# Retention's output rows and six attention tiles turned by DMA instead of by TensorE

## What is computed

```
ret = retention(rq, rk, rv, rg, pos)        # 4 heads of 128 -> columns 0..511
att = mla(c_q, c_kv, k_pe, ...)             # 4 heads of 128 -> columns 512..1023
x = x + concatenate([ret, att]) @ w_o
h = rmsnorm(x); x = x + (silu(h @ w_gate) * (h @ w_up)) @ w_down
...
# in mla, per head and block of 128 queries, keys up to the query's chunk:
prob = softmax(mask(q_blk @ k^T * scale));  out = prob @ v
```

## Time and profile before

| what | value |
|---|---|
| median of 3 runs | 1220.97 us (1220.86 to 1221.05) |
| the profiled execution's own time | 1221.42 us |
| its span | 1219.8 us |
| TensorE busy | 1209.0 us, 99% |
| VectorE, ScalarE, GpSimd busy | 60%, 40%, 49% |
| granted TensorE clock, mean | 0.999 |

### The profile page before, as it was taken

One profiled execution on the slowest core, in us unless ns is written; L12 is line 12 of the kernel. 1 busy time (PEld: TensorE's weight loads), 2 busy tenths in 40 slices (PEclk: granted clock), 3 DMA queues, 4 the chain that ended last, 5 costly groups with the idle time before them and its releaser, 6 DMA issues.

```text
span 1219.8 us, 16374 instructions
## 1 busy us (share of the span) xinstructions
PE 1209.0 (99%) x5842; PEld 1022.4 (84%) x5842; DVE 731.4 (60%) x1160; ACT 487.4 (40%) x882; POOL 594.7 (49%) x586
## 2 busy tenths in 40 slices
PE   9999999999999999999999999999999999999997
PEld 8888888889998888888888888888888888888886
DVE  5654554476664258645554445544499999967634
ACT  6633333355653135433333333333344334525422
POOL 3567775550010024535543355533499889939211
PEclk9999999999999999999999999999999999999999
DMA  9534322100034200423333233332554555434202
GB/s 338 164 86 79 93 42 61 23 18 18 19 121 139 52 1 1 136 80 123 97 119 102 80 121 99 118 104 78 182 194 158 184 173 190 123 104 84 70 35 104
DMA packets 144239, 125.37 MB, mean 103 GB/s; under 512 B 47008, under 2 KB 110112, under 8 KB 144160
## 3 DMA queue, kind: packets, MB, share of 16 engines
q1 hardware_dynamic: 143728, 123.80, 33.5%
q10 hardware_dynamic: 432, 0.54, 0.2%
HBM read 90.49 MB, written 23.59 MB: 94 GB/s over the span
## 4 chain that ended last, share of the span: by engine, by line
PE 95%; DVE 1%; POOL 1%; ACT 1%; issue 1%; DMA 0%; POOLq 0%; SPq 0%; DVEq 0%; ACTq 0%
PE PS L1816 11%; PE PS L1818 11%; PE PS L1817 11%; PE PS L208 8%; PE PS L210 8%; PE PS L209 8%; PE PS L2151 5%; PE PS L2152 5%; PE PS L2150 5%; PE PS L1120 4%; PE PS L1150 3%; PE PS L2571 2%; PE PS L2573 2%; PE PS L2572 2%; PE PS L2586 2%; PE PS L954 1%
## 5 line engine op out<-in xcount | busy, mean ns | idle before, releaser
L208 PE MATMUL PS<-WF,HTH 128*128 128x512 f32 (+1 forms) x448 | 176.7, 394 | 1.1 <-DVE WF L186 0.8
L210 PE MATMUL PS<-WF,HTL 128*128 128x512 f32 (+1 forms) x448 | 173.1, 386 | 0.0
L209 PE MATMUL PS<-WF,HTH 128*128 128x512 f32 (+1 forms) x448 | 173.0, 386 | 0.0
L1537 DVE TENSOR_TENSOR X<-X,PS 128x512 f32<-128x512 f32 x172 | 110.0, 679 | 51.8 <-PE PS L210 37.2
L1816 PE MATMUL PS<-HTH,WF 128*128 128x512 f32 x336 | 130.7, 389 | 0.0
L1817 PE MATMUL PS<-HTL,WF 128*128 128x512 f32 x336 | 130.7, 389 | 0.0
L1818 PE MATMUL PS<-HTH,WF 128*128 128x512 f32 x336 | 130.7, 389 | 0.0
L1749 DVE TENSOR_TENSOR WF<-RAW,WF 128x512 fp32r<-128x512 f32 x63 | 68.7, 1091 | 77.5 <-ACT WF L1739 77.5
L208 PEld LDWEIGHTS PS<-WF,HTH 128*128 128x128 f32 x448 | 84.2, 188 | 17.0 <-issue 0.8
L1816 PE MATMUL PS<-WF 128*128 128x512 f32 x252 | 98.0, 389 | 0.0
L1817 PE MATMUL PS<-WF 128*128 128x512 f32 x252 | 98.0, 389 | 0.0
(11 more groups left out here) (276 smaller groups left out, 2826.6 us busy)
## 6 DMA issues: line engine op xcount, KB each, us to landing
hid<-TMP SPq DMA_DIRECT2D x74, 256.0 KB, 2.3
TMP<-hid SPq DMA_DIRECT2D x25, 512.0 KB, 4.4
RAW<-in_w_ffn_gate SPq DMA_DIRECT2D x22, 512.0 KB, 4.2
RAW<-in_w_ffn_up SPq DMA_DIRECT2D x22, 512.0 KB, 5.4
RAW<-in_w_ffn_down SPq DMA_DIRECT2D x22, 512.0 KB, 4.3
X<-in_x SPq DMA_DIRECT2D x16, 512.0 KB, 5.7
RAW<-in_w_in SPq DMA_DIRECT2D x32, 256.0 KB, 4.3
TAB<-hid SPq DMA_DIRECT2D x9, 512.0 KB, 4.4
```

What stands on the lines that cost most here:

```text
L208: nc.tensor.matmul(dst, HTH[:, k, tok], w_h, start=(k == 0), stop=False)
L209: nc.tensor.matmul(dst, HTH[:, k, tok], w_l, start=False, stop=False)
L210: last = nc.tensor.matmul(dst, HTL[:, k, tok], w_h, start=False, stop=(k == K - 1))
L1537: nc.vector.tensor_tensor(x, x, src, ALU.add).then_inc(done, 1)
```

## The change

Tiles 6 and 7 of heads 0, 1 and 2 (`by_dma`) are no longer turned by TensorE. GpSimd sorts their words' halves into planes (`late_split`), SP issues a DMA transpose into the one buffer JUNK (`sp_late`), and GpSimd joins them into `P_LATE` (`late_join`); the second DMA waits for the first join, as both land in JUNK. Their values are made in steps 3 and 5 of the next head (`VALUES_AT`). `act_exp` of the next head's tiles 0 and 1 now waits for those two splits instead of for a turn. Retention's eight tiles go the same way through GpSimd and SP, one after the other: three at head 0, one each at heads 1 and 2, three at head 3 (`RET_AT`), each time ahead of that head's `out_weights_lo` in GpSimd's order. Their splits into high part and rest read SBUF instead of PSUM and begin in step 3 of the last head. The first output product stands before the values of tile 30, and the output products use six PSUM banks instead of four. SP issues the second half of `w_o` and the reload of `x` later.

```diff
+        RET_AT = ((0, 1, 2), (3,), (4,), (5, 6, 7))
...
+            head_weights(0)
+            for h in range(HEADS):
+                for t in RET_AT[h]:
+                    sp_retention_turn(e, t)
+                if h < HEADS - 1:
+                    head_weights(h + 1)
+                    sp_late(e, h * T + T - 2)
+                    sp_late(e, h * T + T - 1)
...
+        def by_dma(n):
+
+            return n < (HEADS - 1) * T and n % T >= T - 2
...
+        def late_split(e, n):
+            h, t = n // T, n % T
+            e.wait_ge(a_prob, 2 * n + 2)
...
+            nc.gpsimd.tensor_copy(halves(late_halves(n)[0]), words_of(tmp((t % 2) * 1024, (t + 1) * P))).then_inc(p_words, 1)
+
+        def sp_late(e, n):
...
+            e.wait_ge(p_words, 4 * h + 1 + 2 * i)
+            planes, turned = late_halves(n)
+            e.dma_start_transpose(blocks(turned), planes).then_inc(p_turned[i], 16)
+
+        def late_join(e, n):
+            h, i = n // T, n % 2
+            e.wait_ge(p_turned[i], LATENTS_IN + 16 * (h + 1))
+            planes, turned = late_halves(n)
+            nc.gpsimd.tensor_copy(words_of(P_LATE[i][:, 0:(n % T + 1) * P]), halves(turned)).then_inc(p_words, 1)
...
+                if n == NR - 1:
+                    out_product(e, 0)
+                for v in VALUES_AT[n]:
+                    pe_values(e, v)
+                if not by_dma(n):
+                    pe_turn(e, n)
+            out_product(e, 1)
             pe_values(e, NR - 1)
-            pe_retention_turn(e, (4, 5))
-            out_product(e, 1)
-            pe_retention_turn(e, (6, 7))
...
             if n >= 2:
-                e.wait_ge(a_turn, n - 1)
+                if by_dma(n - 2):
+                    e.wait_ge(p_words, 4 * ((n - 2) // T) + 1 + n % 2)
+                else:
+                    e.wait_ge(a_turn, turns_before(n - 1))
...
             for h in range(HEADS):
+                for t in RET_AT[h]:
+                    retention_turn(e, t)
                 out_weights_lo(e, h)
...
+                if h < HEADS - 1:
+                    late = (h * T + T - 2, h * T + T - 1)
+                    for n in late:
+                        late_split(e, n)
+                    for n in late:
+                        late_join(e, n)
...
+        def retention_turn(e, t):
...
+            nc.gpsimd.tensor_copy(halves(RET_HALVES), words_of(RET[:, t])).then_inc(rt_words, 1)
+            e.wait_ge(rt_turned, 16 * (t + 1))
+            nc.gpsimd.tensor_copy(words_of(RET[:, t]), halves(RET_HALVES_T)).then_inc(rt_words, 1)
...
-            return bank(4 + n % 4 if n >= T else (6, 4, 5, 7)[n % 4])
+            return bank(4 + n % 4 if n >= T else (2, 3, 4, 5, 6, 7, 2, 3)[n])
...
             if n == 0:
                 e.wait_ge(o_w_lo, HEADS)
-                e.wait_ge(a_o_lo, NR - 1)
```

More of the change, by code:

```diff
@@ L1138, in pe_values @@
                 e.wait_ge(a_vh, 1)
[L1139 to L1142, removed]
-            else:
-                e.wait_ge(a_pt, n + 1)
-            if n >= 2:
-                e.wait_ge(a_o_lo, n - 1)
+            p = VALUE_PLACE[n]
+            if p < 2:
+                e.wait_ge(b_qr, 7 + p)
+            if by_dma(n):
+                e.wait_ge(p_words, 4 * h + 3 + n % 2)
+            elif t >= 4:
+                e.wait_ge(a_pt_left, turns_before(n + 1, 4))
+            else:
+                e.wait_ge(a_pt, turns_before(n + 1))
+            if p >= 2:
+                e.wait_ge(a_o_lo, p - 1)
+            turned = P_LATE[n % 2] if by_dma(n) else PT[t % 2]
             for j in range(t + 1):
-                if j == 4:
-                    e.wait_ge(a_pt, n + 1)
-                last = nc.tensor.matmul(bank(6 + t % 2, P), value_part(h, j), PT[t % 2][:, j * P:j * P + P], start=(j == 0),
+                if j == 4 and not by_dma(n):
+                    e.wait_ge(a_pt, turns_before(n + 1))
+                last = nc.tensor.matmul(value_bank(n), value_part(h, j), turned[:, j * P:j * P + P], start=(j == 0),
                                         stop=(j == t))
@@ L1205, in act_out_hi, with turned_copy @@
             h, t = n // T, n % T
-            e.wait_ge(a_pv, n + 1)
-            nc.scalar.copy(HTH[:, h + 4, t * P:t * P + P], bank(6 + t % 2, P)).then_inc(a_o_hi, 1)
+            e.wait_ge(a_pv, VALUE_PLACE[n] + 1)
+            nc.scalar.copy(HTH[:, h + 4, t * P:t * P + P], value_bank(n)).then_inc(a_o_hi, 1)
+        def turned_copy(e, n):
+            t = n % T
+            before = [m for m in range(n) if not by_dma(m) and m % 2 == n % 2]
+            if before:
+                e.wait_ge(a_pv, VALUE_PLACE[before[-1]] + 1)
+            left = min(t + 1, 4) * P
+            right = (t + 1) * P - left
+            if right:
+                e.wait_ge(a_turn_left, turns_before(n + 1, 4))
+                nc.scalar.copy(PT[t % 2][:, 0:left], bank(4)).then_inc(a_pt_left, 1)
+            e.wait_ge(a_turn, turns_before(n + 1))
+            dst, src = (PT[t % 2][:, left:left + right], bank(5, right)) if right else (PT[t % 2][:, 0:left], bank(4, left))
+            nc.scalar.copy(dst, src).then_inc(a_pt, 1)
         def act_3b(e):
@@ L1218, in act_3b @@
                     queries_hi(e, h + 1, t // 2)
[L1219 to L1224, removed]
+                for v in VALUES_AT[n]:
+                    act_out_hi(e, v)
                 if t in (4, 5):
                     out_weights_hi(e, h, t - 4)
[L1227 to L1239, removed]
+                if not by_dma(n):
+                    turned_copy(e, n)
+                if last_head and t >= 3:
+                    act_retention_hi(e, [t - 3])
             act_out_hi(e, NR - 1)
-            act_retention_hi(e, range(4, T))
+            act_retention_hi(e, range(5, T))
         def dve_biggest(e, n):
@@ L1286, in dve_3b @@
                     queries_lo(e, h + 1, t // 2)
[L1287 to L1293, removed]
+                for v in VALUES_AT[n]:
+                    dve_out_lo(e, v)
+                if last_head and t >= 3:
+                    dve_retention_lo(e, [t - 3])
             dve_out_lo(e, NR - 1)
-            dve_retention_lo(e, range(4, T))
+            dve_retention_lo(e, range(5, T))
         def pool_3b(e):
@@ L1303, in pool_3b, with sp_retention_turn @@
             for h in range(HEADS):
+                for t in RET_AT[h]:
+                    retention_turn(e, t)
                 out_weights_lo(e, h)
[L1307 to L1313, removed]
+                if h < HEADS - 1:
[4 more added lines that the diff above has]
+                        late_join(e, n)
+        RET_HALVES, RET_HALVES_T = (RAW[:, c:c + HALF].bitcast(U16) for c in (2048, 3584))
+        def retention_turn(e, t):
+            if t == 0:
+                e.wait_ge(r_done, NR)
+                e.wait_ge(b_w_lo, 2)
+            nc.gpsimd.tensor_copy(halves(RET_HALVES), words_of(RET[:, t])).then_inc(rt_words, 1)
+            e.wait_ge(rt_turned, 16 * (t + 1))
+            nc.gpsimd.tensor_copy(words_of(RET[:, t]), halves(RET_HALVES_T)).then_inc(rt_words, 1)
+        def sp_retention_turn(e, t):
+            e.wait_ge(rt_words, 2 * t + 1)
+            if t == 0:
+                e.wait_ge(b_qh, T)
+                e.wait_ge(b_qs, T)
+            e.dma_start_transpose(blocks(RET_HALVES_T), RET_HALVES).then_inc(rt_turned, 16)
         def act_retention_hi(e, tiles):
             for t in tiles:
-                e.wait_ge(rt_turned, t + 1)
+                e.wait_ge(rt_words, 2 * t + 2)
+                e.wait_ge(a_scores, NR - T + t + 1)
                 nc.scalar.copy(HTH[:, 0:4, t * P:t * P + P],
-                               bank((t + 2) % 4).rearrange("p (k n) -> p k n", k=4)).then_inc(rt_hi, 1)
+                               RET[:, t].rearrange("p (k n) -> p k n", k=4)).then_inc(rt_hi, 1)
         def dve_retention_lo(e, tiles):
```

73 lines of the change are left out of this document (41 added, 32 removed).

## The result

The changed kernel takes 1236.47 us (median of four executions, 1233.76 to 1237.44), the kernel before 1221.01; the ratio is 1.0122, 95% interval 1.0109 to 1.0134. It is slower by 15.5 us, and 1235 was forecast. The profiled execution is the fastest of the four, 1233.76 us with a span of 1232.0, 12.2 above the span of before.

A forecast was written before the change was run, and what follows sets the result against it. TensorE, busy 99% of the span, bounds the kernel; 10.9 (product's start) + 0.9 (work behind it) + 2.2 (clock) = +14.0, the removed 7.7 already inside, on median 1220.97 gives 1235 us. Range 1228 to 1240, with margin 1227 to 1241.

The forecast's parts named there:

- The bound and the saving: On TensorE, busy 99% of the span: removed turns save 7.7 us, 4.4 from late tiles and 3.3 from retention.
- Prices: GpSimd's copies and DMA landings, read between two sizes: a retention tile takes split 1.04, landing 3.1, join 1.34 us.
- The seams: At three head ends, tile 3's scores wait for an exponential behind GpSimd's split: 2.45 us idle, 0.9 net loss each.
- The lock's 0.5: At a head's end, tile 6's split waits for tile 7's division at the port VectorE and GpSimd share: 0.5 us.
- The product's start: First output product waits for GpSimd's chain of 38.7 us: TensorE idles 11 to 12 us, start 10.9 later.
- 2.0 for the lock: In GpSimd's chain into the first output product, copies held up by VectorE at the shared port: 2.0 us.
- The clock: After the long wait at the first output product, TensorE restarts at a lower clock: up to 2.2 us.
- the forecast 14.0: Whole kernel slower by 14.0 us: 10.9 for the product's later start, 0.9 for work behind it, 2.2 for the clock.
- What costs nothing: Retention's high parts and rests, later x loads and late tiles' values: covered by TensorE's wait or in time, no cost.
- (a): Rival: GpSimd is in time for the first output product, only head ends idle: 1220.5 us, no change, chance 0.05.
- (c): Rival: the port lock delays divisions throughout the heads, so TensorE's turns come late: +5, 1240 us, chance 0.12.

The follow-up runs named there:

- experiment 3: Changed kernel with only retention's tiles by DMA, attention tiles 6 and 7 turned by TensorE as before: 1219.45 us, ratio 0.9985.
- experiment 6: Changed kernel with late splits ahead of the rest of w_o and, in the last head, that rest ahead of retention's tiles 6 and 7: 1217.05 us, ratio 0.9965.
- experiment 8: Changed kernel with only the late tiles by DMA, retention turned by TensorE as before, late splits ahead of the rest of w_o: 1219.63 us, ratio 0.9988.
- experiment 5: Changed kernel with GpSimd splitting both late tiles ahead of the rest of w_o in the first three heads: 1228.08 us, ratio 1.0058.
- experiment 1: Changed kernel with the last head's rest of w_o made ahead of retention's tiles 6 and 7 on GpSimd: 1225.36 us, ratio 1.003.
- experiment 7: Changed kernel with unused identity matmuls filling TensorE's idle places, 9 at each of three seams and 44 before the first output product: 1232.07 us, ratio 1.0089.
- experiment 2: Changed kernel with 38 unused identity matmuls where TensorE waits for the first output product: 1234.6 us, ratio 1.0102.
- experiment 9: Changed kernel with retention's tile 5 moved from head 3 to head 2 in GpSimd's and SP's order: 1232.22 us, ratio 1.0086.

## Why the prediction was right, point by point

- **The bound and the saving.** TensorE bound, and the turns are gone. That 7.7 us of work are worth 7.7 is what experiments 3, 6 and 8 correct: 1.7 of 3.3, 4.0 of 7.7 and 1.4 of 4.4 arrived, as turns had also covered waits.
- **Prices.** A retention tile's copies took 1.04 to 1.53 and 1.34 us and its landing 3.1 (4.85 once), against 1.04, 1.34 and 3.1; a late tile's joins 2.2 and 2.5 to 2.8. Prices read off a line between two sizes held.
- **The seams.** Forecast 2.45, taken as 2.4; measured 2.17, 1.90, 1.90. The chain held: the split was to end at 321.1 and the exponential at 321.75, and the scores began at 321.48. The lock's 0.5 came too, but as a longer instruction: the split's record starts at 318.73, inside a division, and lasts 2.14 (the longest of L1137; the two records make 3.97), against 1.68 in experiment 5, where no division was in its way. Most of the 0.5 by which the idle time fell short is GpSimd's subtraction, 2.37 instead of 2.65 at the last two seams (the first, with 2.65, idled 2.17), and the modelled end of the scores before, 319.58, which is 0.15 past the place where the next matmul would have begun. Experiment 5 shows the cause as argued.
- **The product's start.** The chain was forecast from 343.5 to 382.15, 38.7 us; it ran from 342.48 to 379.80, 37.3. I had put 2.0 for the lock, and about 1.6 came: 2.14 for the first split instead of 1.68, 2.73 for the second join instead of 2.51, 1.50 and 1.53 for two of retention's splits instead of 1.04. The rest of the difference is mostly the two subtractions, 2.37 and 2.34 instead of 2.65, and records that overlap by 0.05 to 0.1 from one copy to the next. The start was 8.6 later than before, not 10.9, and the wait 8.9, not 11 to 12. Experiments 1 and 5 show it to be GpSimd's order.
- **The clock.** Forecast 2.2 us at the product, measured 2.8. The row that the 2.2 came from does not show the clock: in the windows from 0 to 8 us of the kernel before, over its first 36 matmuls, the profile gives a granted clock of 1.00. The size was near by luck. That it could fall at the seams too was missed: I had taken only the long gap into account. Experiment 7 puts all of the clock's cost at 4.4 to 5 us in the median. This missed term and the too long wait cancel: the profiled execution was 12.2 slower, 1.8 less than the forecast 14.0, and the median is 2.7 above it. That 1235 is nearer to 1236.5 than its terms were to theirs is luck; the wait at the product, its cause and its place in the sum are not.
- **What costs nothing.** It held in the changed kernel, where TensorE waited anyway, and cost 1.5 us once the cover was gone, in experiment 3.
- **Rivals.** (a) would have been the outcome with the edit of experiment 1 but for the clock and small waits (1225.4 instead of 1220.5). (c): divisions do run up to 2.71 us, against 1.19 before, yet in the changed kernel only its weight loads waited for one, 0.2 us. The rule of the Trainium skill ("SBUF — State Buffer", section on SBUF's two separate sides) that one instruction blocks the other in full agrees with this row of experiment 6. Its longest division, 2.81 us from 329.00, has 640 elements, which took 0.55 from 304.68 and from 353.22; it ran beside GpSimd's join from 328.95 to 331.47 and ended 0.34 after it. The split at 318.73 agrees as well, by the 0.46 us that it took longer:

```profile
L1329 DVE TENSOR_SCALAR TMP<-TMP,ST x32: 354/699/2814, 274.2 to 367.0; 128x128 f32<-128x128 f32 x4, 128x256 f32<-128x256 f32 x4, 128x384 f32<-128x384 f32 x4, 128x512 f32<-128x512 f32 x4
```

## What to carry to other kernels

An engine with 84 us of waiting is not free for work in any order: ask what stands behind each of its rare instructions, and when it must have got there. Work moved to it goes behind the instruction that another engine waits for, unless what is moved is waited for sooner; here four such places decided between 1.2% slower and 0.35% faster. And count for every new idle place of TensorE not only its length but the slow matmuls behind it.

## What the runs showed of the hardware

- Idle places of 1.9 to 2.2 us were followed by a low clock in some executions and not in others, though the programs are the same up to there: behind the first and second seam in the profile of experiment 1, behind the third alone in that of the changed kernel, behind all three in that of experiment 2. Each such drop cost 1.6 to 1.7 us. The 9 us gap was followed by it in both profiles that left it idle (0.50 in the changed kernel and in experiment 5), and so were the 3.45 us of experiment 9 (0.60) and the 2.1 us of experiment 2 (0.77). This is the main source of scatter from 1233.8 to 1237.4 in a kernel whose predecessor's four executions beside it scatter by 0.2.
- A VectorE or GpSimd instruction held up by the other shows in the profile as one that starts inside the other and lasts longer: a division of 1024 elements begun 0.35 us before the end of GpSimd's subtraction (318.44, 0.90 us) and one begun 0.63 before it (343.73 in the kernel before, 1.18 us) both ended 0.55 after it.
- The first output product ran at a pitch of 0.43 us per matmul of 128x512 with the clock at 0.50, and 0.23 at 1.00, so the clock's two levels show in the pitch almost as 2 to 1.
- A DMA transpose of 8 blocks let GpSimd go on 3.10 to 3.13 us after its split, time after time. Right behind two loads of `w_o` it took 3.56, 3.62 and 5.19 (experiment 3). The 4.85 of the changed kernel had no such load ahead of it, and its cause is open.
